# One DMA of 2 MB with 16 KB rows for each expert matrix, where there were two of 1 MB with 8 KB rows

## The reference, cut to what matters

```python
def expert_block(args):
    xb, e = args
    hid = jax.nn.silu(xb @ w_gate[e]) * (xb @ w_up[e])
    return hid @ w_down[e]
```

## Time and profile before

| | us |
|---|---|
| median of 3 runs (2630.91 to 2641.88) | 2632.75 |
| the profiled execution | 2641.32 |
| its span in the profile | 2639.3 |
| TensorE busy | 2333.8 (88%) |
| VectorE busy | 1881.3 (71%) |
| ScalarE busy | 1552.8 (59%) |
| GpSimd busy | 283.3 (11%) |

### The profile page before, as it was taken

How to read it: one execution, slowest core, us unless ns; L and a number is a source line. 1 busy time by engine, 2 the same in 40 slices (tenths; PEclk the granted TensorE clock), 3 DMA queues, 4 the chain that set the end, 5 groups by cost and what they waited for, 6 DMA issues and landing times. The chain is left out here.

```text
span 2639.3 us, 34467 instructions
## 1 busy us (share of the span) xinstructions
PE 2333.8 (88%) x11464; PEld 1760.4 (67%) x11464; DVE 1881.3 (71%) x2461; ACT 1552.8 (59%) x2036; POOL 283.3 (11%) x260
## 2 busy tenths in 40 slices
PE   7899989569999999929999999998965999999991
PEld 5666658447777767627777777776854777777661
DVE  6775572668889888858556666556256889888884
ACT  5554460447777777725555565555043778777772
POOL 0000020012121111030000000002001122211102
PEclk9999999779999999959999999998977999999996
DMA  3013021469999999852000000002145999999995
GB/s 120 25 48 102 24 72 32 170 230 398 396 393 394 400 395 395 326 173 88 25 24 24 24 24 24 0 25 71 32 170 205 390 393 400 398 394 393 399 354 211
DMA packets 129501, 538.48 MB, mean 204 GB/s; under 512 B 23232, under 2 KB 52032, under 8 KB 80288
## 3 DMA queue, kind: packets, MB, share of 16 engines
q1 hardware_dynamic: 110496, 470.62, 47.0%
q0 software_dynamic: 18944, 67.12, 7.3%
HBM read 487.50 MB, written 50.20 MB: 204 GB/s over the span
## 5 line engine op out<-in xcount | busy, mean ns | idle before, releaser
L1501 DVE TENSOR_TENSOR m_lo_gate<-m_raw_gate,m_hi_gate 128x2048 fp32r<-128x2048 f32 x132 | 299.4, 2291 | 84.1 <-ACT m_hi_gate L1496 82.4
L1501 DVE TENSOR_TENSOR m_lo_up<-m_raw_up,m_hi_up 128x2048 fp32r<-128x2048 f32 x128 | 292.6, 2286 | 7.9 <-ACT m_hi_up L1496 7.9
L1496 ACT CAST m_hi_down<-m_raw_down 128x2048 fp32r<-128x2048 f32 x124 | 236.1, 1906 | 93.9 <-DMA m_raw_down<-in_moe_w_down_dram 58.4
L1501 DVE TENSOR_TENSOR m_lo_down<-m_raw_down,m_hi_down 128x2048 fp32r<-128x2048 f32 x124 | 280.6, 2285 | 15.1 <-ACT m_hi_down L1496 15.1
L1496 ACT CAST m_hi_gate<-m_raw_gate 128x2048 fp32r<-128x2048 f32 x132 | 248.0, 1906 | 34.5 <-DMA m_raw_gate<-in_moe_w_gate_dram 34.4
L1496 ACT CAST m_hi_up<-m_raw_up 128x2048 fp32r<-128x2048 f32 x128 | 244.4, 1911 | 23.6 <-DMA m_raw_up<-in_moe_w_up_dram 23.5
L1616 PE MATMUL m_G<-m_hi_gate,m_x_hi 128*96 128x512 f32 x512 | 206.6, 404 | 12.2 <-DVE m_x_lo L1726 11.5
L1616 PE MATMUL m_U<-m_hi_up,m_x_hi 128*96 128x512 f32 x512 | 205.2, 401 | 0.0
L1617 PE MATMUL m_G<-m_hi_gate,m_x_lo 128*96 128x512 f32 x512 | 204.8, 400 | 0.0
L1618 PE MATMUL m_G<-m_lo_gate,m_x_hi 128*96 128x512 f32 x512 | 202.9, 396 | 0.0
L1617 PE MATMUL m_U<-m_hi_up,m_x_lo 128*96 128x512 f32 x512 | 201.8, 394 | 0.0
(11 more groups left out here) (380 smaller groups left out, 4917.4 us busy)
## 6 DMA issues: line engine op xcount, KB each, us to landing
m_raw_gate<-in_moe_w_gate_dram SPq DMA_DIRECT2D x128, 1024.0 KB, 12.0
m_raw_up<-in_moe_w_up_dram SPq DMA_DIRECT2D x128, 1024.0 KB, 12.9
m_raw_down<-in_moe_w_down_dram SPq DMA_DIRECT2D x124, 1024.0 KB, 12.0
out_rows<-m_y POOLq DMA_DIRECT2D x64, 384.0 KB, 7.5
a1n_rows<-in_diff_w_qkv_dram SPq DMA_DIRECT2D x21, 512.0 KB, 5.3
out_rows<-a0n_gain SPq DMA_DIRECT2D x1, 8064.0 KB, 36.9
x_res<-in_x_dram SPq DMA_DIRECT2D x4, 1024.0 KB, 9.7
a0n_rows<-in_swa_w_o_dram SPq DMA_DIRECT2D x8, 512.0 KB, 3.4
```

Of the source, the lines that this page charges most:

```text
L1496: act.copy(self.hi[w][:, cut], self.raw[w][:, cut]).then_inc(self.hi_done[w], 1)
L1501: eng.tensor_tensor(self.lo[w][:, cut], self.raw[w][:, cut], self.hi[w][:, cut].bitcast(F32), ALU.subtract)\
```

## The change

Each matrix comes with one DMA over the whole raw buffer (rows of 16 KB) and one semaphore. The casts and subtractions stay in two pieces, and both casts wait for the one semaphore. Before it starts a load, SP waits for both subtractions of the buffer. The order of matrices on SP is the same. The number of DMAs for expert weights goes from 384 to 192, the bytes stay.

```diff
-                for piece in range(2):
-                    moe.load(sp, 0, piece, 0)
+                moe.load(sp, 0, 0)
                 norm.sync_store(sp)
                 for w in range(1, 3):
-                    for piece in range(2):
-                        moe.load(sp, w, piece, 0)
+                    moe.load(sp, w, 0)
...
                 for w in range(2):
                     for piece in range(2):
-                        act.wait_ge(moe.raw_loaded[w][piece], 16)
+                        act.wait_ge(moe.raw_loaded[w], 16)
                         moe.high_part(act, w, piece)
...
-        self.raw_loaded = [[s(f"{w}_loaded_{piece}") for piece in range(2)] for w in names]
+        self.raw_loaded = [s(f"{w}_loaded") for w in names]
...
-        sp.dma_start(self.raw[to][:, cut], rows[:, cut]).then_inc(self.raw_loaded[to][piece], 16)
+        sp.dma_start(self.raw[to][:, :], rows).then_inc(self.raw_loaded[to], 16)
...
-                    def load(w, piece, b, expert):
-                        sp.wait_ge(lo_done[w], 2 * b + piece - 1)
-                        self.load(sp, w, piece, expert)
+                    def load(w, b, expert):
+                        sp.wait_ge(lo_done[w], 2 * b)
+                        self.load(sp, w, expert)
...
-                    for piece in range(2):
-                        sp.wait_ge(lo_done[0], 2 * last + 1 + piece)
-                        self.load(sp, 2, piece, expert, 0)
+                    sp.wait_ge(lo_done[0], 2 * last + 2)
+                    self.load(sp, 2, expert, 0)
...
                     def split(w, b, piece, first=False):
-                        act.wait_ge(self.raw_loaded[w][piece], 16 * (b + 1))
+                        act.wait_ge(self.raw_loaded[w], 16 * (b + 1))
```

More of the change, by code:

```diff
@@ L1479, in __init__, with load @@
         names = ("gate", "up", "down")
-        self.raw_loaded = [[s(f"{w}_loaded_{piece}") for piece in range(2)] for w in names]
+        self.raw_loaded = [s(f"{w}_loaded") for w in names]
         self.hi_done, self.lo_done = ([s(f"{w}_{n}") for w in names] for n in ("hi_done", "lo_done"))
         self.hi, self.lo = ([sb(f"{name}_{n}_{w}", [P, KD * HIDDEN], F32R) for w in names[:2]] for n in ("hi", "lo"))
-    def load(self, sp, w, piece, expert, to=None):
+    def load(self, sp, w, expert, to=None):
         to = w if to is None else to
         k = KH if w == 2 else KD
-        cut = slice(piece * PIECE, (piece + 1) * PIECE)
         rows = self.weights[w][expert].rearrange("(p k) n -> p (k n)", k=k) if isinstance(expert, int) else \
             self.weights[w][bass.ds(expert, 1)].rearrange("e (p k) n -> p (e k n)", k=k)
-        sp.dma_start(self.raw[to][:, cut], rows[:, cut]).then_inc(self.raw_loaded[to][piece], 16)
+        sp.dma_start(self.raw[to][:, :], rows).then_inc(self.raw_loaded[to], 16)
     def high_part(self, act, w, piece):
@@ L1555, in _ @@
                     for w in range(3):
-                        for piece in range(2):
-                            load(w, piece, 1, 1)
+                        load(w, 1, 1)
                     second = expert_of(2)
                     for w in range(2):
-                        for piece in range(2):
-                            load(w, piece, 2, second)
+                        load(w, 2, second)
                     with sp.Fori(2, last) as b:
@@ L1564, in _ @@
                         for w in range(2):
[L1565 to L1568, removed]
+                            load(w, b + 1, following)
+                        load(2, b, expert)
                     expert = expert_of(last)
-                    for piece in range(2):
-                        sp.wait_ge(lo_done[0], 2 * last + 1 + piece)
-                        self.load(sp, 2, piece, expert, 0)
+                    sp.wait_ge(lo_done[0], 2 * last + 2)
+                    self.load(sp, 2, expert, 0)
                 @block.gpsimd
```

## The result

The changed kernel takes 2652.07 us in the median (4 runs, 2650.38 to 2657.66), the kernel before 2633.24 us beside it. The ratio is 1.0059, with a 95% interval of 1.0041 to 1.0076. The profiled execution took 2657.66 us (span 2655.8; the earlier trace rows belong to one of 2639.3). The forecast was 2625 us, between 2616 and 2638.

The account below looks back on a forecast made before the run. Expert blocks were bound by TensorE at 17.63 us, then by DMA at 17.85 to 17.94. From the profiled 2641.32 us, 2 (loops) and 6 (first gathers) came off, giving 2633.3; 8 us off the median gave 2625, range 2616 to 2638.

Parts of the forecast that it names:

- 24 x 0.008 = 0.19 us less of DMA work in a block: Expert loops: 24 weight packets per engine instead of 48, each packet with about 0.008 us fixed; a gain of 2 us.
- The rule of turns: An engine alternates between queues packet by packet, so first-gather packets wait behind weight packets; whole gain 4 us, not 8.
- What bounds the loops: Expert loops: TensorE's floor of 17.63 us a block first, then the DMA's 17.85 to 17.94 once the weights' lead is gone.
- the 5.6 us: Everything a faster DMA can win inside both expert loops, over 14 and 8 DMA-bound blocks, before TensorE's floor holds.
- Landing and release in whole matrices: Loads in the expert loops: later casts and reissue leave the DMA queue supplied, 0 us, but cost 2.5 to 5 us of lead.
- The first gather: Start of each expert stage: 2 MB of loads compete instead of 3, so it lands 3 us earlier; two stages, 6 us.
- C: Rival, chance 0.10: a 16 KB packet is slower than two of 8 KB; at 2% slower +21 us, 2654.
- D: Rival, chance 0.05: buffers turn over late and the DMA engines run dry in the loops; +9 to +26 us, 2642 to 2659.
- E: Rival, chance 0.12: the gather gains 5.2 us in each stage and the loops run at TensorE's floor; -16 us, 2617.
- G: Rival, chance 0.06: each stage's first gather stands behind 16 KB packets and gains only 1.1 us; -4 us in all, 2629.
- F: Rival, chance 0.01: much of a DMA's cost is fixed, so 192 fewer win a lot; at most 5.6 us in the loops.
- B: Rival, chance 0.20: a 16 KB row costs what two of 8 KB cost; +9.8 - 6 = +4 us, 2637.

Follow-up runs that it names:

- e9: e5 with each 1 MB piece loaded by two DMAs of 4 KB rows; 17.95 and 18.08 us a block in the two layers.
- e5: e2 with the third matmul of each product and most of each subtraction left out; 2605.82 us, ratio 0.9875 to the kernel before.
- e8: e6 with gathers and stores cut to 16 rows after block 0; 2485.32 us, blocks of 15.59 and 15.57 us.
- e6: The changed kernel with the third matmul of each product and most of each subtraction left out; 2619.45 us, ratio 0.9929 to the kernel before.
- e11: The changed kernel run again without an edit; 2655.63 us, ratio 1.0064 to the kernel before.
- e2: Kernel before, keeping two 8 KB-row DMAs per matrix, but both issued after both subtractions and both casts waiting for both halves; 2644.88 us, ratio 1.0026.
- e3: Kernel before with only the release changed: both DMAs of a matrix issued after both its subtractions; 2636.70 us, ratio 0.9994.
- e4: Kernel before with only the landing changed: both casts of a matrix wait for both halves; 2643.02 us, ratio 1.0019.
- e1: The kernel before run again without an edit, as a control; 2637.50 us, ratio 0.9994.

## Why the prediction was wrong

It failed at one step, "24 x 0.008 = 0.19 us less of DMA work in a block". The packet's 0.616 us was right when it moves alone, but the step left the other 2.9 us of a block, most of which belong to gathers and stores, as they were. They grew to 3.3 (e9's table, 12 x 0.24 to 12 x 0.27). What grew is the time of the weight packets themselves: beside the busy queue they last 4.9% longer with 16 KB rows and 2.4% with 8 KB (e5 to e8). So the pace went up by 0.25 us (e5 to e6) where I had it fall by 0.19. I had weighed the sharing of the queues for the first gather alone, where it is 1 or 2 us once, and not for the 62 blocks in which both queues run at once. The time that the loops spend above TensorE's floor (31 x 17.63 us a layer) I put at 3.6 us; it is 19 in the first profile and 23 in e11.

The rule of turns that I cited from the Trainium skill ("DMA: Bandwidth & Descriptors", section "Queues, rings and completion order") is borne out by how long a gather takes in the loop: 7.6, 8.9 and 11.2 us from issue to landing beside rows of 4, 8 and 16 KB (e9, e5, e6). But in 700 to 1000 us of these loops TensorE never stands idle for a gather, so that wait costs nothing by itself; the loss of pace comes from weight packets that last longer, which taking turns alone doesn't give.

The other steps, in order:

- *What bounds the loops*, TensorE at 17.63 us and the DMA at about 17.85, and a lead that is eaten: right. (The second layer has nine bound blocks and not eight, the last ending at 2565.70 us; that makes the 5.6 us 5.8.) e2, e3 and e4 move the switch between the two and leave both paces.
- *Landing and release in whole matrices*: right that the queue doesn't run dry (DMA share 1.00 and 1.01) and that the price is the lead. For the case without a cheaper packet I had 9.8 us in the loops; e2's are 10.3 us longer than e1's (553.6 + 552.2 against 547.9 + 547.6), and 6.9 longer than those of the profile that I worked from (549.6 + 549.3). I had laid it to landing and release alike; e3 and e4 show that the landing costs most of it.
- *The first gather*: right mechanism, too large. I took 3 us a stage; the profile after has 2.3 and 1.4, e11 about 2 against e1. The size of the rows has no part in it: with 8 KB rows and the same 2 MB beside it (e2) the gather takes 8.7 and 8.3 us, with 16 KB rows 8.3 to 9.0.
- *The rivals*: the case that came is C's, with a chance of 0.10. By C's own prices a packet 1.7% dearer in effect (0.25 us a block over 24 packets, on 0.624) gives +4 + 15 = +19 us; the medians differ by 18.8. That the two agree so closely is luck, as C was told of the packet alone, and there it is not slower at all. D and E didn't happen: the DMA share never fell, and the loops never ran at the floor. G had its mechanism in the wrong place: gathers wait longer behind 16 KB packets in the loop (9.8 us before, 11.1 after), but not at the start of a stage. F shows nowhere; the 2 us for a DMA that it quotes from the Trainium skill are given there for DMAs issued from GpSimd, and these are SP's. B is what e2 is, with the gather's gain: +4 forecast, +6.4 measured.

By the ratios, whole matrices account for 0.26 of the 0.6%, and the packet beside the other queue for the rest (e6 over e5 gives 0.5%, somewhat more than the 0.33 to 0.38 that are left; there the DMA sets the pace of every block). The loops say the same: the changed kernel's in e11 are 10.6 us longer than e2's, 0.4% of the whole. Why weight packets last longer beside the other queue, and the larger ones more so, and whether the gather or the store does it, stays open; no run separates them.

## What to carry to other kernels

Where the DMA engines bound a loop and two queues share them, the time of a packet alone may not give the pace, as here: take the pace of the loop less the weight packets, and expect that rest to change with the size of the packets. Where two limits lie within 1 or 2% of each other, what a change does to the lead of one over the other counts as much as what it does to either. And look at the start of a stage: a small transfer that everything waits for belongs ahead of the large ones that nobody needs yet.

## What the runs showed of the hardware

- Packets of 4, 8 and 16 KB alone take 0.160, 0.311 to 0.312 and 0.616 us on one engine, a straight line with about 0.008 us fixed. Beside gathers and stores of 4 KB rows in another queue the order of 8 and 16 KB turns round (17.82 and 18.07 us a block), and turns back when the other queue is nearly quiet (15.68 and 15.59). What lengthens beside the busy queue is the weight packets, by 2.4% with 8 KB rows and 4.9% with 16 KB rows.
- A gather in the loop lands 7.6, 8.9 and 11.2 us after its issue beside weight rows of 4, 8 and 16 KB.
- A DMA share of 1.01 with 396 GB/s and one of 1.01 with 392 GB/s look alike. A full share said that the engines had packets, not that they moved bytes at their best.
- A gather of 96 rows takes 5.2 us beside nothing, 8.3 to 9.0 beside 2 MB of weights in the same engines and 10.1 to 10.6 beside 3 MB.
